# Query tiles, gates and output parts moved between the steps of the last attention of a two-block model

## The chip, the cores and the metric

The kernel runs on one core of a Trainium2 chip. The time is the device time of one execution in microseconds (us). TensorE multiplies matrices, VectorE, ScalarE and GpSimd do elementwise work, and SyncE (SP) and ScalarE issue the transfers. In the profile TensorE is PE (its weight loads PEld), VectorE DVE, ScalarE ACT, GpSimd POOL.

## The reference, cut to what matters

Two transformer layers of one model are followed by an mLSTM layer and an attention layer of a second one, all in fp32 on 512 tokens of width 1024 and 256 context tokens. The change touches the last layer alone, the attention `attn_mixer` (no context output is needed there):

```python
q, k, v, z = split(h @ w_in)               # 16 query heads, 4 key heads, of 64
q, k = rms_norm(q) , rms_norm(k)           # per head, with gains
ql, kl = rope(ql) * scale, rope(kl)
s_loc = where(|qpos - kpos| <= 128, ql @ kl.T, -inf)
s_ctx = ql @ kc.T                          # 256 context keys
p = softmax over [s_loc, s_ctx, sink]      # the sink adds to the sum alone
y = (p @ [v, vc]) * silu(z) @ w_out
x = x + gate * y
```

## The kernel before

Every engine has a program of its own, written out in order, and waits on semaphores that count what the other engines have finished; `at(engine, name)` is the count that stands for a named event, `claim` makes TensorE wait until the last reader of a PSUM bank is done. A projection in fp32 is three fp32r matmuls (high by high, high by low, low by high part), so each unit of weights (128x1024) is loaded by SP, rounded to its high part by ScalarE (`split`, L1293) and subtracted to its low part by GpSimd (L2778). Three units of split weights are held at a time (`SPLIT_SLOTS`): a split waits until TensorE has used the third unit before it.

The attention has four groups g, one for each key head, and 16 steps r in a group: step s = 16 g + r takes one head and one block of 128 queries (four heads of one block in a row). In step s TensorE computes the scores of unit s (L1237, L1238), transposes the probabilities of unit s-3 (L1253), and in every fourth and first step multiplies four units by the values (L632, fp32) and spreads the reciprocals (L1245). VectorE adds the mask and takes the row minimum (L2721), ScalarE takes the exponential with its row sum (L1984); the transposed probabilities are copied out of PSUM by VectorE for even units (L2739) and by ScalarE for odd ones (L1998). `gated` on VectorE (L2698 to L2706) multiplies the spread reciprocal, the value product and the gate. The sink exponential comes once in four steps (L2729, L1991), its sum and reciprocal at L2748 to L2752.

Into these steps `fill` on TensorE and `follow` on ScalarE and VectorE weave the next group's preparation. In groups 0 to 2 and for n = g+1 they are: four query tiles of 128 tokens (`AQ_STEPS` 0, 1, 2, 4; 24 matmuls of 256 columns each), the key turns (steps 5 and 9), two gates of 512 columns in halves of four k-tiles (`AZ_STEPS` 6, 8, 9, 10), and four query turns (`QT_STEPS` 13, 14, 14, 15; L1162). A query tile is copied by ScalarE (L1827), squared, summed, scaled head by head on VectorE (L2620) and rotated in three parts on all four tiles at once (L2589 to L2596); the turned queries and keys are split into high (L1856, L1850) and low part (L2642, L2633). A gate's silu is made of a copy and an exponential on ScalarE (L1868, L1871), an add of one on GpSimd (L2965), logarithm and exponential on ScalarE (L1878, L1880), and a product on GpSimd (L2971). In group 3 the first half of the output projection fills steps 1, 2, 4, 5, 6, 8, 9, 10 (`AO_STEPS`), for which ScalarE and GpSimd make the high and low part of the gated output (L1886, L2989). After step 63 the second half of the output projection follows.

GpSimd's order for group n is: second unit of gate n, first of query n+1, two adds, second of query n+1, two products, first unit of gate n+1; in the last round the units of the output projection take the place of query and gate n+1, and after it come four low halves of the gated output.

## Time and profile before

| | |
|---|---|
| median of 3 runs | 2458.07 us (2456.03 to 2459.13) |
| profiled execution, its own time | 2458.86 us |
| its span, first to last instruction | 2457.1 us |
| mean granted clock of TensorE | 0.991 |
| last attention, first score to last matmul | from 2164.9 to about 2453.9 us |

The span is what the trace shows; the device time lies 1.8 us around it. A busy time of PE counts the pipelined end of each matmul, so the distance from start to start is what a matmul costs in a row. A granted clock of 1.00 is 2.4 GHz, 0.50 is 1.2 GHz, and a share in between means that a window holds both.

### The profile page before, as it was taken

The numbers are of one execution on the slowest core, as the hardware profiler recorded it, in microseconds if no ns is written. First come the engines' busy times: TensorE is split into PE (matmuls) and PEld (weight loads), VectorE is DVE, ScalarE is ACT, GpSimd is POOL, SyncE is SP. The second block draws the span as 40 slices with busy tenths as digits, with TensorE's granted clock in tenths as the row PEclk, the third lists the DMA queues.
The fourth block names the chain that finished last, engine by engine and source line by source line (L and its number), as shares of the span: only waits on it lengthen the run. The fifth ranks groups of instructions, "written<-read, shape, count | busy, mean of one in ns | idle before, by whom it ended". The sixth has DMA issues, their size and how long they took to land.

```text
span 2457.1 us, 32452 instructions
## 1 busy us (share of the span) xinstructions
PE 2397.0 (98%) x12352; PEld 2002.5 (81%) x12352; DVE 1302.2 (53%) x2362; ACT 1019.5 (41%) x1789; POOL 955.6 (39%) x519
## 2 busy tenths in 40 slices
PE   9999999999999999999999999999999999999998
PEld 8877788888888678888888888888888888887766
DVE  5466588631255667875026733831462552656563
ACT  5564544432345544444334323331322332464552
POOL 5232444765523235466653223222323224331231
PEclk9999999999999999999999999999999999999999
DMA  5212255222321124632321111121111111211100
GB/s 199 69 39 78 103 180 189 96 94 95 137 64 53 69 78 154 205 121 99 105 95 52 61 44 52 52 69 61 52 60 44 52 52 52 64 52 35 35 18 35
DMA packets 54585, 200.48 MB, mean 82 GB/s; under 512 B 6176, under 2 KB 6176, under 8 KB 53664
## 3 DMA queue, kind: packets, MB, share of 16 engines
q1 hardware_dynamic: 52272, 189.27, 22.8%
q10 hardware_dynamic: 2160, 9.15, 1.1%
q8 instruction: 99, 1.62, 0.3%
q14 instruction: 54, 0.44, 0.1%
HBM read 196.29 MB, written 2.10 MB: 81 GB/s over the span
## 4 chain that ended last, share of the span: by engine, by line
PE 87%; DVE 6%; ACT 3%; issue 2%; POOL 1%; DMA 0%; SPq 0%; DVEq 0%; ACTq 0%; POOLq 0%
PE ps L582 28%; PE ps L909 25%; PE ps L602 18%; PE ps L632 7%; PE ps L1040 2%; PE ps L800 2%; PE ps L1253 1%; DVE arena L2072 1%; PE ps L816 1%; POOL wl L2778 1%; DVE ps L2050 1%; PE ps L1238 0%; PE ps L1237 0%; ACT kh L1417 0%; DVE arena L2296 0%
## 5 line engine op out<-in xcount | busy, mean ns | idle before, releaser
L2778 POOL TENSOR_TENSOR wl<-wring,wh 128x1024 fp32r<-128x1024 f32 (+1 forms) x305 | 735.5, 2412 | 1169.0 <-ACT wh L1293 1137.1
L1293 ACT ACTIVATE wh<-wring 128x1024 fp32r<-128x1024 f32 (+1 forms) x305 | 316.5, 1042 | 429.2 <-PE ps L909 223.9
L582 PE MATMUL ps<-hh,wh 128*128 128x512 f32 x768 | 300.1, 391 | 2.2 <-POOL wl L2778 2.2
L582 PE MATMUL ps<-hh,wl 128*128 128x512 f32 x768 | 298.8, 389 | 0.0
L582 PE MATMUL ps<-hl,wh 128*128 128x512 f32 x768 | 298.8, 389 | 0.0
L602 PE MATMUL ps<-hh,wh 128*128 128x512 f32 (+1 forms) x472 | 200.2, 424 | 5.7 <-DVE hl L2759 2.4
L602 PE MATMUL ps<-hh,wl 128*128 128x512 f32 (+1 forms) x472 | 187.5, 397 | 0.0
L602 PE MATMUL ps<-hl,wh 128*128 128x512 f32 (+1 forms) x472 | 186.6, 395 | 0.0
L582 PEld LDWEIGHTS ps<-hh,wh 128*128 128x128 f32 x768 | 144.1, 188 | 33.9 <-DVE arena L2287 1.7
L582 PEld LDWEIGHTS ps<-hl,wh 128*128 128x128 f32 x768 | 144.2, 188 | 30.5 <-issue 0.5
L582 PEld LDWEIGHTS ps<-hh,wl 128*128 128x128 f32 x768 | 144.1, 188 | 29.8
L1580 ACT ACTIVATE arena<-ps,prmt 128x512 f32<-128x512 f32 x88 | 68.6, 779 | 226.7 <-DVE ps L2050 226.7
L632 PE MATMUL ps<-arena 128*128 128x64 f32 (+2 forms) x624 | 138.4, 352 | 11.3 <-DVE arena L2256 4.6
L909 PE MATMUL ps<-hh,wh 128*128 128x512 f32 x368 | 144.3, 392 | 0.0
L909 PE MATMUL ps<-hl,wh 128*128 128x512 f32 x368 | 144.3, 392 | 0.0
L909 PE MATMUL ps<-hh,wl 128*128 128x512 f32 x368 | 143.1, 389 | 0.0
L582 PE MATMUL ps<-gu_h,wh 128*128 128x512 f32 x352 | 137.2, 390 | 0.0
L582 PE MATMUL ps<-gu_h,wl 128*128 128x512 f32 x352 | 137.0, 389 | 0.0
L582 PE MATMUL ps<-gu_l,wh 128*128 128x512 f32 x352 | 136.9, 389 | 0.0
L1531 ACT ACTIVATE arena<-arena,st 128x128 f32<-128x128 f32 (+3 forms) x128 | 71.8, 561 | 139.8 <-DVE st L2227 139.0
L2072 DVE CUSTOM_DVE_ANT_0 arena<-arena,ps 128x1024 f32<-128x1024 f32 x96 | 117.3, 1222 | 13.9 <-DVE mod L2072 0.3
L632 PEld LDWEIGHTS ps<-arena 128*128 128x128 f32 x624 | 88.0, 193 | 37.6 <-issue 20.2
(373 smaller groups left out, 5613.2 us busy)
## 6 DMA issues: line engine op xcount, KB each, us to landing
wring<-wts SPq DMA_DIRECT2D x290, 512.0 KB, 3.4
arena<-wts SPq DMA_DIRECT2D x48, 512.0 KB, 4.0
wring<-wts SPq DMA_DIRECT2D x16, 384.0 KB, 3.0
xL<-xt SPq DMA_DIRECT2D x4, 512.0 KB, 6.8
arena<-tab SPq DMA_DIRECT2D x1, 2048.0 KB, 16.4
arena<-cv ACTq DMA_DIRECT2D x2, 1024.0 KB, 4.9
arena<-tab ACTq DMA_DIRECT2D x1, 2048.0 KB, 9.8
out_t<-xL ACTq DMA_DIRECT2D x8, 256.0 KB, 2.0
```

Of the source, the lines that this page charges most:

```text
L582: mm = nc.tensor.matmul(o[0], a, b, start=start and k == first and j == 0, stop=stop and k == last and j == 2)
L602: mm = nc.tensor.matmul(dst, a, b, start=start and x == 0 and i == 0 and j == 0, stop=stop and x == len(us) - 1 and i == kn - 1 and j == 2)
L632: last = nc.tensor.matmul(dst, a, b, start=start and i == 0, stop=stop and i == len(pairs) - 1)
L800: last = nc.tensor.matmul(ps[:, s % 3, 0:ke], a, b, start=x == 0, stop=x == len(bs) - 1 and kind != "fox")
L816: last = nc.tensor.transpose(ps[:, 3 + tb, 128 * j:128 * j + 128], sbuf[:, u % 4, 128 * j:128 * j + 128], idn)
L909: mm = nc.tensor.matmul(dst, a, b, start=x == 0 and i == 0 and j == 0, stop=x == len(us) - 1 and i == kn - 1 and j == 2)
L1040: last = nc.tensor.matmul(l, x, y, start=s == 0 and i == 0, stop=s == NA - 1 and i == 2)
L1293: nc.scalar.activation(wh[:, sn % SPLIT_SLOTS, :kn * w], raw(u)[:, :kn * w], ACT.Copy).then_inc(act_done, tick("act", ("hi", u)))
L1531: nc.scalar.activation(sbuf[:, s % 4, 0:ke], sbuf[:, s % 4, 0:ke], ACT.Exp, scale=-1.0, bias=mx1[:, s % 16:s % 16 + 1], accum_out=rs1[:, s ...
L1580: nc.scalar.activation(yb[:, m % 3, :], ps[:, up_bank(m), :], ACT.Identity, scale=conv[:, l, 2, m:m + 1], bias=conv[:, l, 3, m:m + 1]).the ...
L2072: V.tensor_tensor_reduce(out=ada_dump, in0=raw(u), in1=silu_c[j], scale=1.0, scalar=0.0, op0=ALU.mult, op1=ALU.add, accum_out=modv[:, laye ...
L2778: G.tensor_tensor(wl[:, sn % SPLIT_SLOTS, :kn * w], raw(u)[:, :kn * w], wh[:, sn % SPLIT_SLOTS, :kn * w].bitcast(F32), ALU.subtract).then_inc(
```

## The change

The work of the last attention is put at other steps, some of it in other pieces; what is computed stays.

- TensorE's query tiles move a group ahead: those of group n+2 stand at steps 9, 10, 13, 14 of group n (bank 6 and 7 in turn). Three tiles of group 1 come before step 0, the fourth in step 0.
- The queries are squared, summed, rooted, rotated, turned and split in two pairs of tiles instead of in one piece or four. Pair 0 is turned at step 8 (9 in group 2), pair 1 at 12. The key turns stand at steps 1 and 5.
- The gates stand at steps 1 to 6; those of the last group are cut into quarters of two k-tiles, at steps 1, 2, 5, 6, 9, 10 of group 2.
- The output projection's first half goes to steps 46, 49, 50, 53, 54, 57, 58, 61, with two banks in turn, and one part of its second half to step 62. Step 46 now waits for the low half 3.
- ScalarE copies the transposed probabilities ahead of the step's exponential instead of behind it.
- Row sum and sink exponential lie side by side in pairs, and one reduction takes the place of the addition.
- GpSimd's order changes with the splits; the product of gate 7 comes behind the four low halves.

```diff
-AQ_STEPS, AZ_STEPS, AO_STEPS = (0, 1, 2, 4), (6, 8, 9, 10), (1, 2, 4, 5, 6, 8, 9, 10)
-QT_STEPS = {13: [(0, 7)], 14: [(1, 6), (2, 7)], 15: [(3, 7)]}
+AZ_STEPS = ({1: ((0, 0, 4),), 3: ((0, 4, 8),), 5: ((1, 0, 4),), 6: ((1, 4, 8),)},
+            {1: ((0, 0, 4),), 2: ((0, 4, 8),), 5: ((1, 0, 4),), 6: ((1, 4, 8),)},
+            {1: ((0, 0, 4),), 2: ((0, 4, 6),), 5: ((0, 6, 8), (1, 0, 2)), 6: ((1, 2, 4),), 9: ((1, 4, 6),), 10: ((1, 6, 8),)})
+AQ_STEPS = {9: (0, 6), 10: (1, 7), 13: (2, 6), 14: (3, 7)}
+AK_STEPS = {1: 0, 5: 1}
+AQ1_BANKS = (6, 4, 5, 6)
+QT_STEPS = ({8: (0, 7), 12: (1, 7)}, {8: (0, 7), 12: (1, 7)}, {9: (0, 6), 12: (1, 7)})
+AO_STEPS = {46: (0, 7), 49: (1, 6), 50: (2, 7), 53: (3, 6), 54: (4, 7), 57: (5, 6), 58: (6, 7), 61: (7, 6)}
...
-        ars = st[:, 112:128]
-        aes = st[:, 128:144]
+        asum = st[:, 112:144].rearrange("p (h x) -> p h x", x=2)
+        ars, aes = asum[:, :, 0], asum[:, :, 1]
...
+            gate_part(0, 1, 0, KT, 7)
+            for t in range(NT - 1):
+                query_tile(1, t, AQ1_BANKS[t])
... TensorE, fill(s)
+                if s == 0:
+                    query_tile(1, NT - 1, AQ1_BANKS[NT - 1])
+                if g < AT_KV - 2 and r in AQ_STEPS:
+                    query_tile(g + 2, *AQ_STEPS[r])
+                if s in AO_STEPS:
+                    m, b = AO_STEPS[s]
                     if m == 0:
                         pe.wait_ge(pool_done, at("pool", "aol", 3))
+                    claim([b], "dve", "xa0", m)
+                    out_part(m, b, 0, ("xa0", m), start=True, stop=True)
+                if s == 62:
+                    pe.wait_ge(pool_done, at("pool", "aol", 5))
+                    begin_out(2)
... ScalarE, follow(s)
+                    if r in AK_STEPS: high_keys(n, AK_STEPS[r], 6)
+                    for i, _, k1 in AZ_STEPS[g].get(r, ()):
+                        if k1 == KT: gate_parts(2 * n + i, 7)
+                    if r == 2: root_of_queries(n, 1)
+                    if r in QT_STEPS[g]: high_queries(n, *QT_STEPS[g][r])
+                if g < AT_KV - 2:
+                    if r in AQ_STEPS: take_query(n + 1, *AQ_STEPS[r])
+                    if r == 3: split(("aq", n + 1), first)
+                    if r == 7: split(("aq", n + 1), second); gate_inverse(2 * n)
+                    if r == 9: split(("az", n + 1), first)
+                    if r == 10: gate_inverse(2 * n + 1)
+                    if r == 11: square_queries(n + 1, 0)
+                    if r == 14: split(("az", n + 1), second)
+                    if r == 15: square_queries(n + 1, 1); root_of_queries(n + 1, 0)
+                elif g == AT_KV - 2:
+                    if r == 3: split(("ao", 0, 0))
+                    if r in (11, 13): high_gated(r - 11); high_gated(r - 10)
+                    if r == 6: split(("ao", 1, 0))
+                    if r == 9: gate_inverse(2 * n)
+                    if r == 10: split(("ao", 2, 0))
+                    if r == 14: gate_inverse(2 * n + 1)
... VectorE, follow(s)
+                    if r == 1: sum_queries(n, 1); scale_queries(n, *range(4))
+                    if r - 1 in AK_STEPS: low_keys(n, AK_STEPS[r - 1], 6)
+                    if r == 2: scale_queries(n, *range(4, 8))
+                    if r == 3: rotate_queries(n, 0, 0)
+                    if r == 5: rotate_queries(n, 0, 1); rotate_queries(n, 0, 2)
+                    if r == 6: scale_queries(n, *range(8, 15))
+                    if r == 7: scale_queries(n, 15)
+                    if r == 10: the three parts of rotate_queries(n, 1, part)
+                    if r - 1 in QT_STEPS[g]: low_queries(n, *QT_STEPS[g][r - 1])
+                if g < AT_KV - 2 and r == 14: sum_queries(n + 1, 0)
...
-                    V.tensor_tensor(arc[:, c4], ars[:, c4], aes[:, c4], ALU.add)
+                    V.tensor_reduce(arc[:, c4], asum[:, c4, :], AX_X, ALU.add)
... GpSimd
+            for n in range(1, AT_KV - 1):
+                add_one(2 * n)
+                split(("aq", n + 1), slice(0, 1))
+                add_one(2 * n + 1)
+                split(("aq", n + 1), slice(1, 2))
+                times(2 * n)
+                split(("az", n + 1), slice(0, 1))
+                times(2 * n + 1)
+                split(("az", n + 1), slice(1, 2))
+            split(("ao", 0, 0)); add_one(6)
+            split(("ao", 1, 0)); times(6)
+            split(("ao", 2, 0)); add_one(7)
             for m in range(4):
                 low_gated(m)
+            times(7)
```

(In the diff some bodies are joined to one line and waits that only guard a buffer are left out.)

## Rows read from the trace of the kernel before

**Rows 1.** The page's head and busy times, whole span.
```profile
span 2457.1 us, 32452 instructions
PE 2397.0 (98%) x12352; PEld 2002.5 (81%) x12352; DVE 1302.2 (53%) x2362; ACT 1019.5 (41%) x1789; POOL 955.6 (39%) x519
```

**Rows 2.** Windows: length, busy us of PE, PEld, DVE, ACT, POOL; clock, DMA, GB/s.
```profile
2211.68:2224.56 12.88, 8.18 (x41) 5.80 (x39) 9.37 (x22) 6.71 (x15) 4.82 (x3) 0.87 0.24 82
2277.95:2292.40 14.45, 9.67 (x41) 6.42 (x39) 9.87 (x22) 7.27 (x17) 4.83 (x3) 0.76 0.20 73
2292.40:2345.25 52.85, 52.29 (x312) 42.42 (x309) 31.51 (x81) 27.82 (x59) 11.18 (x6) 1.00 0.06 21
2345.25:2360.04 14.79, 10.53 (x41) 6.83 (x39) 10.82 (x22) 9.05 (x20) 8.64 (x6) 0.66 0.20 72
2411.21:2422.40 11.19, 8.51 (x47) 5.77 (x45) 5.59 (x15) 3.61 (x9) 0.00 (x0) 1.00 0.00 0
2435.85:2457.10 21.25, 15.64 (x61) 12.32 (x60) 8.15 (x12) 1.48 (x2) 2.40 (x1) 0.92 0.26 99
```

**Rows 3.** Chain of work, parts of the last attention: start, us, what.
```profile
2205.35 0.17 PE ps L1237
...
2208.20 0.12 PE ps L1237
...
2209.12 0.55 PE ps L1253 x5
2209.67 2.59 PE ps L632 x6
...
2228.73 2.87 PE ps L602 x24
...
2402.12 2.76 PE ps L602 x12
```

**Rows 4.** Waits of PE from 2110 us on: us in total, times, longest.
```profile
PE ps L1162 <- DVE norm_sq L2596: 7.0, 3, 2.3
PE ps L1253 <- ACT arena L1998: 5.5, 6, 1.5
```

**Rows 5.** Groups of DVE by form from 2110 us on: busy, mean ns; idle before.
```profile
L2721 DVE CUSTOM_DVE_ANT_0 arena<-ps,arena,st 128x640 f32<-128x640 f32 x32 | 28.2, 881 | 22.9 <-PE ps L1238 13.1 <-PE ps L1245 9.7
...
L2620 DVE SCALAR_TENSOR_TENSOR norm_sq<-norm_sq,st,prmt 128x64 f32<-128x64 f32 x64 | 13.1, 278 | 0.7 <-ACT st L1844 0.6
...
L2698 DVE TENSOR_TENSOR arena<-ps,arena 128x256 f32<-128x256 f32 x16 | 6.7, 420 | 9.5 <-PE ps L1245 9.5
...
L2633 DVE TENSOR_TENSOR akl<-ps,akh 64x512 fp32r<-64x512 f32 x8 | 5.5, 687 | 7.6 <-ACT akh L1850 7.4
...
L2748 DVE TENSOR_TENSOR st<-st 128x4 f32<-128x4 f32 x16 | 2.4, 152 | 0.0
...
L2651 DVE TENSOR_REDUCE st<-arena 128x8 f32<-128x512 f32 x1 | 0.7, 675 | 0.0
```

**Rows 6.** Groups of ACT by form from 2110 us on.
```profile
L1293 ACT ACTIVATE wh<-wring 128x1024 fp32r<-128x1024 f32 x25 | 26.2, 1050 | 12.2 <-PE ps L582 6.5 <-PE ps L602 5.6
...
L1868 ACT ACTIVATE arena<-ps 128x512 f32<-128x512 f32 x6 | 3.6, 599 | 10.3 <-PE ps L602 10.3
```

**Rows 7.** Groups of POOL by form from 2110 us on.
```profile
L2778 POOL TENSOR_TENSOR wl<-wring,wh 128x1024 fp32r<-128x1024 f32 x25 | 60.5, 2418 | 217.9 <-ACT wh L1293 217.5
L2965 POOL TENSOR_SCALAR arena<-arena 128x512 f32<-128x512 f32 x6 | 11.5, 1923 | 29.7 <-ACT arena L1871 29.7
```

**Rows 8.** Timeline of POOL, then of DVE: start, us, what, idle before.
```profile
2255.05 2.36 POOL L2778 TENSOR_TENSOR wl<-wring,wh 128x1024 fp32r<-128x1024 f32 x1 [33.90 <-ACT wh L1293]
...
2354.88 4.09 POOL L2989 TENSOR_TENSOR hl<-arena,hh 128x512 fp32r<-128x512 f32 x3
...
2255.07 2.36 DVE L2729 TENSOR_TENSOR st<-st 128x4 f32<-128x4 f32 x1
...
2279.54 1.56 DVE L2595 TENSOR_TENSOR norm_sq<-norm_sq,norm_tmp 128x512 f32<-128x512 f32 x1
```

More of the change, by code:

```diff
@@ L1165, in gate_half, with query_tile @@
-            def gate_half(g, i, half, b):
+                    for t in range(2):
+                        last = nc.tensor.transpose(ps[:, b, 256 * x + 128 * t:256 * x + 128 * t + 128],
+                                                   atq[:, 2 * pair + t, 128 * x:128 * x + 128], idn)
+                last.then_inc(pe_done, tick("pe", ("qt", g, pair)))
+            def query_tile(g, t, b):
+                us = views(("aq", g))
+                claim([b], "act", "aq", g, t)
+                product(ps[:, b, 0:256], lat_toks(t), us, ("aq", g, t),
+                        *([("used", x[0]) for x in us] if t == NT - 1 else []))
@@ L1895, in _ @@
                 take_query(0, t, t)
-            square_queries(0)
+            for pair in range(2):
+                square_queries(0, pair)
             split(("akv", 1), first)
@@ L1899, in _ @@
                 take_kv(0, x)
-            root_of(aqs, ("qss", 0), "qrs", 0)
+            for pair in range(2):
+                root_of_queries(0, pair)
             take_kv(0, 3)
@@ L1919, in _ @@
             high_keys(0, 1, 1)
-            for t in range(NT):
-                high_queries(0, t, 2 + t)
+            for pair in range(2):
+                high_queries(0, pair, 2 + pair)
             split(("aq", 1), second)
@@ L1932, in follow @@
                         split(("ao", 3, 0))
-                    if r == 6:
+                    if r in (5, 6):
+                        high_gated(r - 1)
+                    if r == 5:
                         split(("ao", 0, 1))
-                        high_gated(4)
-                        high_gated(5)
-                    if r in (9, 11):
-                        split(("ao", (r - 7) // 2, 1))
-                    return
-                n = g + 1
-                ahead = ([(("aq", n + 1), first), (("aq", n + 1), second), (("az", n + 1), first)] if n < AT_KV - 1
-                         else [(("ao", j, 0), slice(None)) for j in range(3)])
@@ new lines, in rotate_queries @@
+            def rotate_queries(g, pair, part):
+                c = slice(2 * pair, 2 * pair + 2)
+                x = nsq_t[:].rearrange("p (t h d) -> p t h d", t=NT, d=64)[:, c]
+                t1, t2 = [atmp[:, i, 256 * pair:256 * pair + 256].rearrange("p (t h d) -> p t h d", t=2, h=4)
+                          for i in range(2)]
+                turn_pairs(x, acos[:, c], asin[:, c], t1, t2, part)
+                if part == 2:
+                    names[("dve", ("qr", g, pair))] = counts["dve"]
```

315 lines of the change are left out of this document (169 added, 146 removed).

## The prediction

> **What bounds the kernel now.** I began with the page's head: TensorE is busy for 2397.0 us of a span of 2457.1 [rows 1], so only work or idle time of TensorE can move the end. That 98% is a mean over stages, and the change touches one, the last attention. I cut it into windows at the score matmuls and set beside each window the time that its matmuls need when they follow each other without a gap. That spacing is read in the chain of work: a score of 256 columns 0.12 us (of 384: 0.17), a transpose 0.11, an fp32 matmul of the value product 0.43 (each is recorded twice, so one key tile costs 0.86), a projection matmul 0.12 at 256 columns and 0.23 at 512 [rows 3].
>
> The windows split the stage clearly [rows 2]. Steps 16 to 28 and 32 to 44 run gapless: the second of them, 52.85 us, has PE busy for 52.29 at clock 1.00. Steps 13 to 15 of groups 0, 1 and 2 begin only 38 matmuls each (the rows count three more that reach over an edge; 12 scores 1.4, 22 transposes 2.4, 4 value matmuls 1.7: 5.6 us), but last 12.88, 14.45 and 14.79 us, at clocks 0.87, 0.76 and 0.66. Together 42.1 us for 16.7 of work: **25.4 us lost**. The waits name the cause: TensorE stands at the query transposes until VectorE has rotated the queries (L1162 on L2596, 7.0 us in three waits), then at the probability transposes for ScalarE's copies (L1253 on L1998, 5.5 us in six) [rows 4], and the half clock of 1.2 GHz that follows stretches the rest. Steps 61 to 63 have the same illness: 44 matmuls that begin there, worth 8.2 us, take 11.19 [rows 2], **3.0 us lost**. So 28.4 us can be had here; matmul work is neither added nor taken away.
>
> **What the change does to each step.** Query tiles and gates were done at steps 0 to 10 of the group that precedes their use, and steps 13 to 15 were left bare. Now the query tiles of group n+2 stand at steps 9, 10, 13, 14, the gates at 1 to 6, the turned queries at 8 and 12. With the spacings above TensorE's steps 0 to 15 of group 1 cost
>
> before: 6.8, 3.8, 3.8, 2.6, 6.1, 1.5, 3.7, 2.9, 6.0, 4.1, 3.9, 2.9, 4.0, 1.2, 1.5, 2.9;
> after: 3.9, 4.1, 3.6, 2.6, 3.2, 4.0, 3.7, 2.9, 3.7, 4.0, 4.0, 2.9, 4.5, 3.9, 3.9, 2.6
>
> (a query tile 24 x 0.12 = 2.87, a gate half 12 x 0.23 = 2.76). They add up to 57.7 and 57.5, the same but for rounding.
>
> Can the others follow? VectorE, step by step, from [rows 5] less the 0.08 by which neighbours overlap: bias and minimum 0.80 at 640 columns (0.68 at 512), a copy about as long, three products of the gated output 1.35 (0.42 each and their waits), reciprocals 0.7; the moved work is sixteen head scalings 0.21 apart, key parts 1.24 and 0.86, rotations, low halves. After: 2.0, 3.4, 2.8, 2.3, 2.2, 3.8, 3.1, 2.0, 2.2, 3.5, 3.3, 1.7, 2.0, 3.4, 1.3, 1.5, in all 40.5: below TensorE at every step, by 0.2 at least. ScalarE was busy for 27.8 and 9.1 us in steps 32 to 47 [rows 2] and does the same work in no more instructions: about 37 of 57. So TensorE stays the bound if nothing stands still in the wrong place, and the 28.4 us are the gross gain. A query tile is moved three times into the stretch ahead of step 0 (8.6 us there, 8.6 less in steps 0 to 2): no sum changes, and the half of the tile's weights that is last split is due about when the first half of tile 0 has run; cost 0, up to 1 us if it is late.
>
> **Forms that the trace does not show.** Half a rotation (128x256, both inputs in SBUF) lies between nothing but issue and the 128x512 of 0.69; by the 64x512 key part of 0.69 and the reduction of half the queries, 0.68 [rows 5], time goes with the elements of a partition, so I take 0.42, 12 instead of 6 of them: +0.7 us of VectorE in a group, hidden under 17 us of room. The pair sums by TENSOR_REDUCE (128x4 from 128x8) lie between the old addition, 0.15, and the 0.68 of a 512-element reduction; being nearest in elements to the former I take 0.16, cost 0, and at the other end 16 x 0.5 = 8 us of VectorE, still hidden. Query halves now go as 64x512 (the key part's 0.69 and ScalarE's like form) in half as many instructions: a small saving off the path. Loads keep their order and their rule (slot free after the low half of five units before) and SP's queue is passed by nothing; the windows show DMA shares of 0.26 at most [rows 2], so the earlier splits of the output weights find them landed; a load that did not would cost its landing time once.
>
> **Where waits come back.** I walked steps 0 to 48 through the three queues.
> Step 5 of group 0: VectorE does a key part and four scalings in step 2 before it minimises step 3, about 3 us late; ScalarE then has exponential 3, gate 2 (1.2) and a split (1.05) in front of the copy of unit 1, for which the transposes of step 5 wait [rows 5, 6]: **2.4 us**, 0 if VectorE is earlier.
> Steps 12 and 28: VectorE's six rotations of pair 1 (step 10) meet GpSimd's split of the next gate's first half, started by ScalarE in step 9. A VectorE op on two SBUF inputs stands still meanwhile: L2729, 4 elements wide, took 2.36 us beside a split that began 0.02 us earlier [rows 8]. So the rotations end 2.4 us late, minimum 11 and copy 8 behind them, and the transposes of step 12 wait 1.1: **2.2 us** in two groups, between 0 and 4.8.
>
> The Trainium skill (SBUF — State Buffer, Who interferes with whom) says that VectorE with two SBUF inputs and a GpSimd instruction that reads SBUF take turns as wholes, and that TENSOR_REDUCE never contends on trn2. The 2.36 us agree with the first; by the second the pair sums would save up to 2.2 us for each old addition that met a split, and the sum would be lower by that; but the addition took 0.15 us on the mean of 16 [rows 5], so by the trace they save nothing.
>
> Step 46: the first output part now waits here for low half 3. After the last gate piece (step 42) come, in GpSimd's order, gate readings on ScalarE 1.2, split 1.05, low split 2.42, add-one 1.92, four low halves at 4.09/3 = 1.36 apart [rows 6 to 8]: 12.0 us. TensorE has 2.9 + 4.5 + 1.0 + 1.0 = 9.4 until then: **2.7 us**. Queued behind it are the scores of step 47 and all else on TensorE. In the tail, behind a wait, the clock was 0.92 and 61 matmuls took 15.6 us where 13.9 are due [rows 2]; a little over half of that 1.7 is added here, **1.0**.
> The subtraction ahead of the sink exponential (L2729, every fourth step) can again fall just behind a split, at step 15 in groups 0 and 1 and at step 7 in group 2: price up to 2.4 each, of which a copy and a transpose pass on part; **1.6** in all.
> Bank 6 is shared by value product, key turn and query tiles, and freed by VectorE about 1.0 us after the product, while TensorE needs it after 0.9 to 1.5: **0.8** over six places.
> Copies ahead of exponentials cost nothing as long as an exponential has its three steps of room; the 0.7 it is delayed is covered by 2.6 us or more of the shortest step.
>
> Sum: 28.4 − 2.4 − 2.2 − 3.7 − 1.6 − 0.8 = 17.7. The profiled execution took 2458.86 us around its span of 2457.1; less 17.7 that is 2441.2. The median of the three runs, 2458.07, lies 0.8 below the profiled execution, so I predict **2440.4**. With none of the new waits 2429.6, with all of them doubled 2451.
>
> **Rivals.** (a) *The waits mostly come back.* VectorE works in order and idles at each gated product until the value product ends (behind which a projection used to stand, and now at steps 0 and 4 none does). If that makes each of three groups lose 3 us more, 2449 to 2451. For it: my margins at bank 6 and 7 are under 1 us. Against: 17 us of room in each group's VectorE.
> (b) *No change that can be told.* A measurement of this kernel tells about 0.2%, 4.9 us. If the bare steps are slow because of the chain score, minimum, exponential, transpose, copy itself, moving matmuls does not help: what steps 13 to 15 gain, steps 0, 4 and 8 lose, which now hold 8.1 us less between them in a group, and we end within 2453 to 2463. Against: step 11 took 2.85 us with the same chain (first scores at 2205.35 and, of step 12, 2208.20 [rows 3]).
> (c) *Slower, by the shared port.* 27 GpSimd ops with two inputs stand in the loop (15 splits, 12 others), and the rotations, scalings and subtractions are now spread over seven steps instead of five, so more of them meet a split. At 2.4 us a meeting that reaches TensorE it is decided from 8 meetings beyond mine; with 12 the time is 2440.4 + 29 = 2469. Against: before, of a group's rotations one was held and reached TensorE, for 0.9 us of 1.56 in step 29 [rows 8].
>
> By the Trainium skill (SBUF — State Buffer, Who interferes with whom) this is the mechanism, and what it makes of the time is the 2469.
>
> **How the numbers follow.** Forecast 0.70 (2432 to 2447), (a) 0.20, (b) 0.04, (c) 0.06. Faster by over 0.2%: 0.90; within: 0.04; slower: 0.06. The range takes the forecast's lower bound short of the no-wait end and most of (a): 2432 to 2450.
>
> **What would show it.** Right: windows at steps 13 to 15 of about 10 us with twice the matmuls and clock near 1.00 (in groups 0 and 1); no wait of TensorE on the rotation; 57 to 60 us for group 1; one wait of TensorE on GpSimd's low half near step 46; waits of transposes on copies at step 5 and 12. Wrong would be: VectorE busy without gaps over a group, long L2729 or rotations beside splits followed by TensorE idle at the same moment, or a wait for query weights ahead of step 0.

## The result, and the profile after

The changed kernel takes 2441.24 us in the median of six runs (2436.94 to 2448.48), beside 2456.98 (2455.28 to 2459.13) for six runs of the kernel before on the same chip: a ratio of 0.9937, 95% interval 0.9922 to 0.9953. The forecast of 2440.4 us, faster, in a range from 2432 to 2450, holds. A later set of five runs (the last experiment) gave a median of 2444.77 (2440.37 to 2448.09), beside 2457.58 for the kernel before; over all eleven it is 2442.57. The gain is 15.7 us by the first set and 12.8 by the later one, where the forecast had 17.7. The profiled execution, 2436.94 us, is the fastest of the eleven, which matters for how its profile is read.

The head and busy times of the page, as [rows 1]:

```profile
span 2435.2 us, 32465 instructions
PE 2382.3 (98%) x12352; PEld 1994.0 (82%) x12352; DVE 1309.6 (54%) x2374; ACT 1017.9 (42%) x1785; POOL 956.8 (39%) x519
```

The share of TensorE is 98% as before, with the same 12352 matmuls, so it says nothing of what was gained. The windows do. Those of the kernel after, in the columns of [rows 2]: steps 13 to 15 of groups 0, 1 and 2, steps 61 and 62, and the last 21.25 us:

```profile
2214.35:2224.46 10.11, 10.11 (x81) 9.39 (x80) 7.04 (x17) 5.82 (x13) 0.62 (x1) 1.00 0.01 2
2273.11:2283.22 10.11, 10.11 (x81) 9.39 (x80) 7.06 (x17) 5.82 (x13) 0.62 (x1) 1.00 0.01 2
2332.14:2344.56 12.42, 9.14 (x46) 7.12 (x44) 6.91 (x17) 6.29 (x12) 4.32 (x4) 0.86 0.00 0
2390.84:2399.40 8.56, 8.54 (x48) 6.90 (x47) 5.28 (x15) 3.40 (x7) 2.39 (x1) 1.00 0.00 0
2413.95:2435.20 21.25, 15.63 (x64) 11.57 (x63) 8.58 (x13) 1.48 (x2) 2.40 (x1) 1.00 0.26 99
```

In groups 0 and 1 the three steps hold 81 matmuls instead of 41 and take 10.11 us instead of 12.88 and 14.45, PE busy throughout at clock 1.00. In group 2 TensorE still stands idle for over 3 us in them, and the clock is 0.86. The waits of TensorE in the whole attention, as [rows 4], show why. Line numbers have moved: in the changed kernel a projection is L608 (L602 before), the value product L638 (L632), a transpose of probabilities L1270 (L1253), its copy L2031 on ScalarE (L1998) and L2809 on VectorE (L2739), a gate's first exponential L1891 (L1871), the low part of queries L2694 (L2642), a low half of the gated output L3047 on GpSimd (L2989) and, in the tail, L2829 on VectorE (L2759).

```profile
PE ps L608 <- POOL hl L3047: 2.6, 1, 2.6
PE ps L638 <- DVE aq_s L2694: 2.4, 1, 2.4
PE ps L608 <- DVE hl L2829: 2.4, 1, 2.4
PE ps L608 <- ACT arena L1891: 2.0, 1, 2.0
PE ps L1270 <- ACT arena L2031: 1.8, 2, 1.5
PE ps L1270 <- DVE arena L2809: 1.5, 3, 0.8
```

No query transpose waits for a rotation any more. In its place stand six smaller causes: step 46 (low half of the gated output), step 43 (value product behind the queries' low part), the tail, step 37 (a gate quarter), step 5, and steps 4, 12 and 28. Three of them were in the forecast (steps 46, 5, and 12 with 28), the tail's wait stood there before as well (L602 on L2759, 2.4 us), and steps 37 and 43 were not foreseen.

With each matmul at the spacings of [rows 3] (and 0.23 for 512 columns) every step has a length without waits; what the trace shows beyond it is called lost. Summed over steps, in us lost:

| | before | after, profiled | after, another execution (experiment 12) |
|---|---|---|---|
| group 0, 1 | 10.5, 10.5 | 3.2, 1.4 | 4.7, 1.4 |
| group 2 | 10.3 | 12.7 | 16.9 |
| group 3 to step 62 | 2.2 | 1.9 | 1.9 |
| from step 63 on | 6.3 | 3.0 | 4.4 |
| all | 39.9 | 22.2 | 29.3 |

From the key turns to the last matmul the stretch took 295.57 us before and 278.37 after: 17.2 less, where the forecast had 17.7. The spans differ by 21.9; the other 4.7 lie ahead of the last attention, at places that the change does not touch, and are no part of its gain: by its first key turn the execution before was that much behind already (it had been at 1.2 GHz for 20.5 us by then, the one after for 6.8).

Nor is all of the 17.2 the change's own. The stretch from the key turns on as a window, in the columns of [rows 2]: before, after, and after in the other execution of the table (the last experiment):

```profile
2157.91:2453.48 295.57, 273.73 (x1457) 214.63 (x1455) 171.39 (x406) 142.66 (x299) 72.31 (x37) 0.96 0.10 34
2153.19:2431.56 278.37, 263.70 (x1456) 209.03 (x1455) 174.65 (x411) 141.07 (x292) 72.91 (x37) 0.99 0.11 36
2157.16:2442.70 285.54, 271.02 (x1456) 214.50 (x1455) 174.58 (x411) 141.00 (x292) 72.75 (x37) 0.96 0.10 35
```

At the same clock as before, 0.96, the change saves 10.0 us; the other 7.2 of the profiled execution come with a clock of 0.99.

### The profile page after: what moved, and what is told of

Read it like the earlier page. It is cut to its first block, busy times and chain, and to the rows that moved or that the text cites. A ratio compares the mean times of both kernels' runs of the same rounds, so it can differ in the third digit from the quotient of the medians.

```text
span 2435.2 us, 32465 instructions
## 1 busy us (share of the span) xinstructions
PE 2382.3 (98%) x12352; PEld 1994.0 (82%) x12352; DVE 1309.6 (54%) x2374; ACT 1017.9 (42%) x1785; POOL 956.8 (39%) x519
## 4 chain that ended last, share of the span: by engine, by line
PE 89%; DVE 6%; ACT 2%; issue 1%; POOL 1%; DMA 0%; DVEq 0%; ACTq 0%; POOLq 0%
PE ps L588 29%; PE ps L915 25%; PE ps L608 18%; PE ps L638 7%; PE ps L1046 2%; PE ps L806 2%; PE ps L1270 1%; DVE arena L2118 1%; PE ps L822 1%; POOL wl L2848 1%; PE ps L1255 1%; PE ps L1254 1%; DVE ps L2096 0%; DVE arena L2342 0%; PE ps L1041 0%
## 5 line engine op out<-in xcount | busy, mean ns | idle before, releaser
L608 PE MATMUL ps<-hh,wh 128*128 128x512 f32 (+1 forms) x472 | 197.8, 419 | 10.2 <-POOL hl L3047 2.6
L608 PE MATMUL ps<-hh,wl 128*128 128x512 f32 (+1 forms) x472 | 186.1, 394 | 0.0
L608 PE MATMUL ps<-hl,wh 128*128 128x512 f32 (+1 forms) x472 | 185.4, 393 | 0.0
L638 PE MATMUL ps<-arena 128*128 128x64 f32 (+2 forms) x624 | 135.0, 346 | 12.1 <-DVE arena L2302 4.5
L638 PEld LDWEIGHTS ps<-arena 128*128 128x128 f32 x624 | 86.7, 191 | 36.9 <-issue 19.1
## 6 DMA issues: line engine op xcount, KB each, us to landing
arena<-tab SPq DMA_DIRECT2D x1, 2048.0 KB, 17.2
```

Source lines behind the costliest of these rows:

```text
L608: mm = nc.tensor.matmul(dst, a, b, start=start and x == 0 and i == 0 and j == 0, stop=stop and x == len(us) - 1 and i == kn - 1 and j == 2)
L638: last = nc.tensor.matmul(dst, a, b, start=start and i == 0, stop=stop and i == len(pairs) - 1)
```

## The experiments

The theory after the result: the bare steps lost time through the rotation that the turns stood for, that is gone, and what is left in the changed kernel are single waits, each with its own late engine or held bank, followed at times by a half-clock stretch. The rival theories, one for each part, stand in the expectations. A single run of a kernel in which such waits are left tells little by its total (the same kernel spreads over 11.5 us, last experiment), so the first seven experiments, one profiled run each, are judged by their waits. The times of the kernel before on the same chips were 2461.1 us (first four, one run), 2457.85 (next four) and 2457.58 (last four).

The expectations set bounds for the stretch from the first key turn to the last matmul. Here it is for each profiled execution, with the part of it in which TensorE was granted 1.2 GHz:

| | stretch, us | at 1.2 GHz, us |
|---|---|---|
| before | 295.57 | 23.9 |
| after | 278.37 | 3.4 |
| 1 e1_copy_behind | 284.39 | 13.7 |
| 2 e2_add | 279.83 | 6.8 |
| 3 e3_high_early | 280.80 | 10.2 |
| 4 e4_low_first | 285.49 | 20.5 |
| 5 e5_quarter_later | 278.53 | 6.8 |
| 6 e6_split_later | 279.91 | 10.2 |
| 7 e7_halves | 279.14 | 10.2 |
| 8 e8_spread | 274.11 | 6.8 |
| 9 e9_low_ahead | 269.81 | 0.0 |
| 10 e10_part_47 | 268.96 | 0.0 |
| 11 e11_short_tiles | 274.63 | 6.8 |
| 12 e12_after_again | 285.54 | 20.5 |

A projection matmul of 512 columns takes 0.43 us at this level instead of 0.23, so up to half of the last column is time lost, and it must come off before two stretches are compared.

**1. The copy behind the exponential again** (e1_copy_behind).

```diff
-                if 0 <= u < nu and u % 2:   # copy of unit s-3, ahead of exponential s
...
+                if 0 <= u < nu and u % 2:   # the same copy, behind the exponential and the sink's
```

> The changed kernel with one part undone: ScalarE's copy of the transposed probabilities stands behind the step's exponential again. Measured is the stretch from the first key turn to the last matmul, 278.4 us in the changed kernel. Theory 1 (the copies' place is worth little, since the moved matmuls now cover a copy that comes late): the stretch stays within 3 us, and TensorE's waits for these copies, 1.8 us in two waits, grow to 5 us at most. Theory 2 (much of the gain comes from this order): the waits for the copies come back in many steps and the stretch grows by 5 us or more.

2445.09 us. The copies are waited for in three places instead of two; in step 5 the wait is 2.28 instead of 1.47 us, longer by the 0.83 of the exponential that now stands in front:

```profile
PE ps L1270 <- ACT arena L2044: 3.6, 3, 2.3
```

One of the others shortens the wait in step 43 from 2.4 to 1.6, so some 1.0 us of waiting is added in all. The stretch grows by 6.0, past theory 2's bound of 5, but the rest of it is clock: in this execution a half-clock stretch of 6.8 us follows step 5 and one of 3.4 lies in the tail. The order of copy and exponential is worth about 1 us of waits, as theory 1 has it.

**2. The addition instead of the reduction** (e2_add).

```diff
-V.tensor_reduce(arc[:, c4], asum[:, c4, :], AX_X, ALU.add)
+V.tensor_tensor(arc[:, c4], ars[:, c4], aes[:, c4], ALU.add)
```

> The changed kernel with one part undone: row sum and sink exponential are added by a two-input addition again instead of a reduction over pairs. Theory 1 (the trace): nothing changes, the stretch from the first key turn to the last matmul stays within 1 us of 278.4; where the addition meets GpSimd's split in step 5 it waits 1.5 us, but the copy behind it waited for the same split anyway. Theory 2 (the Trainium skill, SBUF - State Buffer, Who interferes with whom: a reduction never contends, two inputs do): held additions reach TensorE and the stretch grows by 1.5 to 3 us.

2440.08 us, and the list of TensorE's waits is that of the changed kernel to 0.1 us. The form itself differs. VectorE's sums by form, this kernel first, then the changed one:

```profile
L2818 DVE TENSOR_TENSOR st<-st 128x4 f32<-128x4 f32 x16 | 4.0, 252 | 0.0
```

```profile
L2818 DVE TENSOR_REDUCE st<-st 128x4 f32<-128x8 f32 x16 | 2.4, 152 | 0.0
```

At the new places one addition of the 16 is held up, in step 5, for 1.74 us instead of 0.15; the reduction never is. But these 1.6 us are not on TensorE's path. That the stretch is 1.5 longer, more than theory 1 allows, goes with a half-clock stretch of 3.4 us behind the wait in step 37, which the profiled execution of the changed kernel does not have there.

**3. The high parts 2 and 3 in step 43** (e3_high_early).

```diff
-                    if r in (11, 13):
-                        high_gated(r - 11)
-                        high_gated(r - 10)
+                    if r == 11:
+                        for m in range(4):
+                            high_gated(m)
```

> The changed kernel, with ScalarE's high parts 2 and 3 of the gated output made in step 43 beside 0 and 1 instead of in step 45. Theory 1 (step 46 waits because GpSimd's low halves 2 and 3 start late behind ScalarE): the wait of TensorE on the low half, 2.6 us, falls below 0.8, the half-clock period behind it goes, and the stretch from the first key turn to the last matmul falls from 278.4 to 273.5 to 276. Theory 2 (GpSimd's own queue of split, add-one and four low halves sets step 46): the wait stays above 1.5 us and the stretch above 276.5.

2440.79 us. GpSimd's four low halves now follow each other without a gap, and the wait for them is gone. But step 46 still waits 1.3 us, which the list puts down to nothing ("issue"). The two timelines name it, TensorE's first and then VectorE's:

```profile
2341.75 0.47 PE L608 MATMUL ps<-hh,wh 128*128 128x512 f32 x1 [1.26 <-issue]
```

```profile
2340.24 1.41 DVE L2694 TENSOR_TENSOR aq_s<-ps,aq_s 64x512 fp32r<-64x512 f32 x2
```

VectorE's low parts of query pair 1 end at 2341.65 and free bank 7; the output part that claims bank 7 begins 0.10 later. The next bound of step 46 is a bank. The stretch was expected at 273.5 to 276 and is 280.8, which misses it: the half clock behind step 46 is gone, but in this execution it follows the waits in steps 37 and 43 and in the tail.

**4. In step 42 the low parts ahead of the rotations** (e4_low_first).

```diff
+                    if r - 1 in QT_STEPS[g]:
+                        low_queries(n, *QT_STEPS[g][r - 1])
                     if r == 10:
                         for part in range(3):
                             rotate_queries(n, 1, part)
-                    if r - 1 in QT_STEPS[g]:
-                        low_queries(n, *QT_STEPS[g][r - 1])
```

> The changed kernel, with VectorE taking the low parts of query pair 0 ahead of the rotations of pair 1 in step 42 instead of behind them. Theory 1 (step 43 waits because bank 6, which the value product needs, still holds the turned queries that VectorE reads after six rotations): the wait of 2.6 us at step 43 falls below 0.5, and the stretch from the first key turn to the last matmul falls by 0.5 to 2.5 us (part is given back at step 46, whose low halves do not come earlier). Theory 2 (the wait is for the probability copies of units 38 and 39): it stays above 2 us.

2444.96 us. The wait in step 43 is gone, and the transposes of step 44 wait 2.5 us instead. The list names ScalarE (L1906); the timeline of VectorE shows the copy of unit 40, which holds the transposes' bank, ending at 2332.32, 0.15 ahead of the transposes, behind the rotations and two instructions that were held:

```profile
2326.11 1.21 DVE L2635 TENSOR_TENSOR norm_tmp<-norm_sq,arena 128x256 f32<-128x256 f32 x1
...
2330.21 1.38 DVE L2799 TENSOR_TENSOR st<-st 128x4 f32<-128x4 f32 x1
2331.51 0.81 DVE L2809 COPY arena<-ps 128x640 f32<-128x640 f32 x1
```

Theory 1 is right on the bank, but the gain that it expected is not there (285.5 us, 20.5 of it at half clock): in either order step 42 puts six rotations, a low part and a copy of VectorE into 2.6 us of TensorE. Two of the rows shown are held beside GpSimd instructions, the rotation of 1.21 us (0.42 for the others) and the subtraction of 1.38 (0.16 at most places). These 2.0 us may be most of the wait; no run here tried that by itself.

**5. The first quarter of gate 7 in step 38** (e5_quarter_later).

```diff
-5: ((0, 6, 8), (1, 0, 2)), 6: ((1, 2, 4),)
+5: ((0, 6, 8),), 6: ((1, 0, 4),)
```

> The changed kernel with one step of the last gates moved: the first quarter of gate 7 is multiplied in step 38 instead of in step 37, where it follows the last quarter of gate 6 in the same PSUM bank 7. Theory 1 (step 37 waits because the bank can only be written again when ScalarE has read gate 6 twice): TensorE's wait of 2.0 us on ScalarE's gate reading goes, and no other wait of steps 36 to 42 grows by more than 0.5. Theory 2 (VectorE is behind in steps 36 to 40 in any case): the wait comes back at the probability transposes of steps 38 to 40, 1.5 us or more.

2436.89 us. The wait of 2.0 us in step 37 falls to 1.0, now in step 38: there too ScalarE reads gate 6 out of bank 7 by copy and exponential before gate 7 may be written. About 1 us is gained in waits, half of what theory 1 expected, and no other wait grows.

**6. The next gate's first split in step 12** (e6_split_later).

```diff
-                    if r == 9:
-                        split(("az", n + 1), first)
...
+                    if r == 12:
+                        split(("az", n + 1), first)
```

> The changed kernel, with ScalarE's split of the next gate's first unit in step 12 instead of step 9 of groups 0 and 1, so that GpSimd's part no longer runs beside VectorE's rotation in step 10. Theory 1 (the shared turn of VectorE and GpSimd delays rotation, copy and the transposes of steps 12 and 28): the first rotation of step 10 takes 0.4 instead of 2.6 us and the waits at steps 12 and 28, 0.55 us each at the transposes, go; the stretch from the first key turn to the last matmul falls by 1 to 2 us, unless the half clock falls otherwise. Theory 2 (these waits come from VectorE's amount of work): the rotation is short, but the waits stay above 0.3 us.

2441.07 us. The first rotation of step 10 in group 0 takes 0.42 us, beside 2.64 in the changed kernel, where GpSimd's split began 0.05 us ahead of it and took 2.41. The timelines of the changed kernel, VectorE and then GpSimd, and of VectorE in this one:

```profile
2204.24 2.64 DVE L2635 TENSOR_TENSOR norm_tmp<-norm_sq,arena 128x256 f32<-128x256 f32 x1
```

```profile
2204.19 2.41 POOL L2848 TENSOR_TENSOR wl<-wring,wh 128x1024 fp32r<-128x1024 f32 x1 [4.70 <-ACT wh L1308]
```

```profile
2206.87 0.42 DVE L2635 TENSOR_TENSOR norm_tmp<-norm_sq,arena 128x256 f32<-128x256 f32 x1
```

The waits in steps 12 and 28 are gone: 0.55 us each. The chain split, rotation, minimum, copy, transpose is shown. The stretch does not fall by the 1 to 2 us expected; it has 10.2 us at half clock instead of 3.4.

**7. The last gates in halves** (e7_halves).

```diff
-1: ((0, 0, 4),), 2: ((0, 4, 6),), 5: ((0, 6, 8), (1, 0, 2)), 6: ((1, 2, 4),), 9: ((1, 4, 6),), 10: ((1, 6, 8),)
+1: ((0, 0, 4),), 2: ((0, 4, 8),), 5: ((1, 0, 4),), 6: ((1, 4, 8),)
```

> The changed kernel with one part undone: the gates of the last group in halves of four k-tiles at steps 33, 34, 37, 38 as in the other groups, instead of quarters up to step 42. Theory 1 (the quarters only shift waits): the 2.0 us at step 37 go, steps 41 and 42 lose 1.4 us of work each and their waits grow by about as much, and the stretch from the first key turn to the last matmul stays within 2.5 us of 278.4. Theory 2 (the quarters carry part of the gain, as they fill steps that VectorE's rotations make long): the stretch grows by 3 us or more.

2441.55 us. Step 37 does not wait any more and step 40 neither, but steps 41 to 43, with the quarters taken out of them, lose 6.8 us instead of 3.2: TensorE waits for ScalarE's copy (2.0) and then for the low part (1.5), with a half-clock stretch of 6.8 us. The stretch of 279.1 is within theory 1's bound. The quarters shift waits; they neither make nor remove them.

**8. All five moves** (e8_spread): edits 3, 5 and 6, the low parts of step 42 ahead of the rotation, the three rotations of pair 1 in group 2 spread over steps 40 to 42, and the split of step 3 in step 4.

```diff
... (of the five moves, the rotations alone)
+                    if r == 10 and g < AT_KV - 2:
+                        for part in range(3):
+                            rotate_queries(n, 1, part)
+                    if 8 <= r <= 10 and g == AT_KV - 2:
+                        rotate_queries(n, 1, r - 8)
```

> The changed kernel with five moves at once: high parts 2 and 3 of the gated output in step 43; in group 2 the three rotations of pair 1 in steps 40, 41 and 42 and the low parts of pair 0 ahead of the last of them; first quarter of gate 7 in step 38; split of the next gate's first unit in step 12 of groups 0 and 1; split of the next query's first unit in step 4 instead of 3. Theory 1 (what is left of the gross gain lies in waits each set by one badly placed instruction: 2.0 at step 37, 0.9 at 40, 2.6 at 43, 2.7 and the half clock behind it at 46, 0.6 each at 12 and 28, about 1 at step 5): the stretch from the first key turn to the last matmul falls from 278.4 to 267 to 272, the median time to 2428 to 2435. Theory 2 (VectorE's and ScalarE's amount of work sets group 2, so that a wait removed comes back in the next step): the stretch stays above 274.

2437.02 us in the median of four (2436.18 to 2437.49), ratio 0.9919 [0.9902, 0.9935]. Theory 1's ranges are missed, 2428 to 2435 by the median and 267 to 272 by the stretch, whose 274.1 lies just above theory 2's bound. The single waits did go: steps 5 and 43 lose 0.9 us at most, steps 12, 28 and 44 next to nothing. What they give is partly lost again in step 46, which TensorE now reaches earlier than GpSimd's low halves:

```profile
PE ps L608 <- POOL hl L3049: 2.9, 1, 2.9
```

With 6.8 us of half clock behind it that step loses 6.7 us, more than the 5.4 of the changed kernel.

**9. As 8, with the low halves ahead of gate 7's add of one** (e9_low_ahead).

```diff
-            add_one(7)
             for m in range(4):
                 low_gated(m)
+            add_one(7)
             times(7)
... ScalarE: gate_inverse(2 * n + 1) of group 2 at r == 15 instead of 14
```

> All five moves, and on GpSimd the four low halves of the gated output ahead of the add of one of gate 7 (1.92 us), whose logarithm and exponential go from step 46 to 47. Theory 1, GpSimd's own chain now sets step 46: its low halves begin 2.2 us sooner, TensorE's wait there falls from 3.1 to about 0.9 us and the half-clock stretch behind it (6.8 us long, 2.7 us lost) goes: 2437.0 - 2.2 - 2.7 = 2432. Theory 2, the wait is passed on to the next engine and the half clock stays: a wait of 1.5 us or more in step 46 or 47, 2435 to 2437.

2432.06 us (2430.29 to 2432.83), ratio 0.9897 [0.9883, 0.9911], as theory 1 has it, and no half clock is left in the stretch. The wait in step 46 is 1.3 instead of the 0.9 expected, and it is not GpSimd's chain but the bank of experiment 3: the low halves end at 2332.49, VectorE's low parts at 2332.81, and the output part begins 0.10 later. From the timelines of GpSimd, VectorE and TensorE:

```profile
2326.93 5.56 POOL L3049 TENSOR_TENSOR hl<-arena,hh 128x512 fp32r<-128x512 f32 x4
```

```profile
2331.40 1.41 DVE L2694 TENSOR_TENSOR aq_s<-ps,aq_s 64x512 fp32r<-64x512 f32 x2
```

```profile
2332.91 0.47 PE L608 MATMUL ps<-hh,wh 128*128 128x512 f32 x1 [1.27 <-POOL hl L3049]
```

**10. As 9, with the first output part in step 47** (e10_part_47).

```diff
-AO_STEPS = {46: (0, 7), 49: (1, 6), ...}
+AO_STEPS = {47: (0, 7), 49: (1, 6), ...}
```

> As the run before, and the first output part in step 47 instead of 46, so that step 46 has one score and its transposes alone (1.0 us). Theory 1, only the low halves hold TensorE there: 1.0 us more room, the wait is gone, 0.9 below the run before, 2431. Theory 2, two bare steps (45, 46) are paid for by the chain score, minimum, exponential, transpose: transposes of steps 47 to 49 wait 1 us or more on an exponential or a copy, and the time is the same as or above the run before.

2431.16 us (2429.44 to 2431.65), ratio 0.9893 [0.9880, 0.9907]: the fastest version, 13.6 us below the changed kernel in the same set of runs (2444.77), though hardly to be told from 9. Of steps 45 to 47 two waits are left, on an exponential (0.7, as in the changed kernel and in 9) and on a copy (0.4). Two bare steps in a row cost only the latter, and the wait on bank 7 is gone: theory 1, though what was waited for was the bank and not the low halves. All steps from 0 on lose 12.7 us.

**11. Short query tiles in steps 13 and 14** (e11_short_tiles): three quarters of the matmuls of tiles 2 and 3 in groups 2 and 3 are left out.

```diff
                 us = views(("aq", g))
+                if g >= 2 and t >= 2:
+                    us = [(u, o, 1, [w[:, 0:1, :] for w in v]) for u, o, n, v in us]
```

> The changed kernel, where query tiles 2 and 3 of groups 2 and 3 (steps 13 and 14 of groups 0 and 1) leave out three quarters of their matmuls (6 instead of 24, so the queries are wrong there): steps 13 and 14 become as bare as before the change, 1.7 instead of 3.9 us of work each, but no rotation is due in them. 4 x 18 x 0.12 = 8.6 us of work are left out. Theory 1, what cost time in the bare steps before was the rotation that the turns stood for and the half clock behind it: all 8.6 us are saved, 2432.5. Theory 2, the chain score, minimum, exponential, transpose, copy cannot go faster than some 3 us a step, and a bare step waits for it: less than half is saved, 2437 or more, with transposes waiting on copies in steps 14 to 17 and 30 to 33.

2437.87 us (2435.01 to 2439.31). Neither theory gives the number. Steps 13 to 15 of groups 0 and 1, in the columns of [rows 2]:

```profile
2217.70:2225.15 7.45, 6.23 (x45) 5.11 (x44) 7.04 (x17) 5.36 (x11) 0.15 (x1) 1.00 0.01 2
2273.81:2281.29 7.48, 6.25 (x45) 5.12 (x44) 7.05 (x17) 5.38 (x11) 0.18 (x1) 1.00 0.00 0
```

They take 7.5 us instead of 10.1, so 5.3 of the 8.6 are saved. The rest is not the waiting of transposes on copies that theory 2 expected; these wait as long as in the changed kernel, 0.8 us in steps 6 to 31. In both groups tile 3 stands until VectorE's low parts of query pair 1 have freed bank 7:

```profile
2222.11 0.38 PE L608 MATMUL ps<-wh,hh 128*128 128x256 f32 x1 [1.22 <-DVE aq_s L2696]
```

So the chain from score to copy does go at 1.8 to 3.4 us a step, and VectorE, busy for 7.04 of 7.45 us, is here the next bound. The bare steps before were not slow by the chain as such; that leaves the rotation due in them, with the copies and exponentials late behind it. Matmuls placed there hide VectorE's work.

**12. The changed kernel once more** (e12_after_again), unaltered.

> The changed kernel unaltered, once more, on the same chip as the three others. Theory 1: median 2441, single runs from 2437 to 2449, and the half-clock stretches stand behind the same waits of 1.6 to 2.7 us (steps 5, 37, 43, 46) but not behind the same ones in every execution. Theory 2: the spread was that of one chip: all runs within 2 us of each other.

2444.77 us in the median of five (2440.37 to 2448.09), ratio 0.9948 [0.9936, 0.9960]. Its profiled execution took 2448.09 us, 11.2 more than the one shown above, and TensorE's waits are the same to 0.2 us. The windows of steps 5, 37 to 38, 43 to 44, 46, and from step 63 on, first of the profiled execution above, then of this one:

```profile
2182.43:2188.16 5.73, 4.26 (x25) 3.60 (x24) 4.53 (x10) 4.53 (x10) 4.32 (x2) 1.00 0.00 1
2299.74:2309.05 9.31, 7.30 (x39) 5.72 (x37) 5.97 (x16) 4.34 (x10) 3.12 (x2) 1.00 0.19 58
2321.64:2332.14 10.50, 7.77 (x38) 4.88 (x36) 7.86 (x14) 7.20 (x15) 7.60 (x5) 1.00 0.15 51
2333.15:2342.33 9.18, 5.90 (x25) 4.59 (x23) 3.97 (x10) 5.00 (x10) 3.81 (x3) 0.81 0.00 0
2397.71:2435.20 37.49, 31.87 (x137) 23.07 (x135) 12.71 (x24) 4.64 (x10) 3.79 (x2) 1.00 0.15 56
```

```profile
2186.42:2193.65 7.23, 5.76 (x26) 4.87 (x24) 5.30 (x13) 4.53 (x10) 4.29 (x2) 0.76 0.11 32
2305.24:2316.13 10.89, 8.88 (x38) 7.08 (x37) 6.36 (x18) 4.35 (x10) 3.12 (x2) 0.84 0.15 50
2328.60:2341.85 13.25, 10.52 (x38) 6.58 (x36) 7.85 (x14) 7.20 (x15) 8.09 (x5) 0.74 0.13 41
2342.87:2351.78 8.91, 5.64 (x24) 4.37 (x23) 3.96 (x10) 5.00 (x10) 3.81 (x3) 0.84 0.00 0
2407.45:2446.40 38.95, 33.26 (x137) 24.12 (x135) 12.71 (x24) 4.64 (x10) 3.78 (x2) 0.96 0.14 54
```

Behind the same waits the clock is 1.00 in one execution and 0.74 to 0.84 in the other in three of the four stretches of steps; step 46 is slowed in both. Theory 1 holds, but for a median 3.8 above its own. The lengths differ by 1.50 + 1.58 + 2.75 − 0.27 + 1.46 = 7.0 us, nearly all of the 7.2 by which the stretch from the key turns to the last matmul is longer (285.54 to 278.37). The other 4 of the 11.2 lie ahead of the attention, where this execution has 17.1 us at half clock and the first 6.8. Experiments 9 and 10, where these waits are gone or down to 1.3 us and only the tail's is as long as before, spread over 2.5 and 2.2 us.

## Why the prediction was right, point by point

**The bound and the gross gain.** The bare steps were to lose nothing once they had work in them, and in groups 0 and 1 that held (steps 13 and 14 lose 0.1 us together). The rotation as the cause held as well: VectorE does it steps ahead, no transpose waits on it, and experiment 11 shows that the steps could even be bare without the chain holding them for as long as before. But up to 10 of the 25.4 us were half clock (20.5 us in steps 14 to 47), and that part need not stay away: the other execution of the changed kernel has as much of it at new places.

**Steps 61 to 63 and the tail.** The 3.0 us predicted in steps 61 to 63 came: with projection matmuls in steps 61 and 62 these two waits of the kernel before are gone.

```profile
2414.44 0.74 PE L1253 MATMUL ps<-prmt,arena 128*128 128x128 f32 x5 [1.18 <-ACT arena L1984]
...
2417.15 0.63 PE L1253 MATMUL ps<-prmt,arena 128*128 128x128 f32 x4 [1.50 <-ACT arena L1998]
```

The loss from step 63 on fell from 6.3 to 3.0; half of this is the second of these waits, and half was not in the forecast: the clock behind the tail's wait (2.4 us as before) is 1.00 instead of the 0.92 of [rows 2]. That half is luck of the execution; in the other one, with the clock at 0.96, the loss is 4.4.

**Step 5.** 2.4 us predicted, by VectorE's late minimum and ScalarE's queue. Measured 1.6 in step 5 and 0.8 in step 4, both behind VectorE's late minimum of step 3: 2.4. (The kernel before lost 0.9 in step 4 too, where the transposes followed those of step 3 with only the scores in between; the gross gain below counts it.)

**Steps 12 and 28.** The mechanism was right in each link (experiment 6), the size twice too large: 0.55 us a group instead of 1.1.

**Step 46.** Predicted 2.7 of wait and 1.0 of clock, by GpSimd's chain without a break. Measured: 0.7 at the transposes, a wait of 2.6, and 1.8 of clock: the spacing of the projection matmuls behind the wait is 0.43 us instead of 0.23. The wait has the right size by luck, and by another path: GpSimd stood idle for 2.5 us between low halves 1 and 2, because ScalarE makes the high parts 2 and 3 only in step 45. The timeline of GpSimd in the changed kernel:

```profile
2329.96 2.69 POOL L3047 TENSOR_TENSOR hl<-arena,hh 128x512 fp32r<-128x512 f32 x2
2335.15 2.68 POOL L3047 TENSOR_TENSOR hl<-arena,hh 128x512 fp32r<-128x512 f32 x2 [2.51 <-ACT hh L1906]
```

Without this gap GpSimd's chain takes the 12.0 us predicted and ends at 2335.3; but TensorE, late from step 43, reached the output part only then, so the chain by itself would have cost nothing. Once the gap and the add of one are out of the way (experiments 3 and 9), bank 7 is next.

**Sink subtraction and bank 6.** 1.6 predicted for the subtraction; measured about 0.9 in step 40, behind a subtraction held for 1.29 us in step 39, one of the places named. 0.8 predicted for bank 6 over six places; measured 0.2 to 0.3 in each of steps 17, 21, 33, 49, 53, 57 and 61, 1.7 in all.

**What was missed.** Two waits that no term of the sum held, both for a PSUM bank whose reader is late. From the timeline of TensorE in the changed kernel, step 37 and step 43:

```profile
2305.14 0.50 PE L608 MATMUL ps<-hh,wh 128*128 128x512 f32 x1 [1.98 <-ACT arena L1891]
...
2325.86 1.95 PE L638 MATMUL ps<-arena 128*128 128x512 f32 x4 [2.41 <-DVE aq_s L2694]
```

In step 37 the last quarter of gate 6 and the first of gate 7 stand back to back in bank 7, so ScalarE must read gate 6 twice in between. In step 43 the value product claims bank 6, which in group 2, and only there, holds the query turn of pair 0 from step 41; VectorE reads it behind the six rotations, one of which is held for 1.1 us (1.50 instead of 0.42) beside GpSimd's product of gate 6. Its row on VectorE's timeline, then GpSimd's:

```profile
2321.97 1.50 DVE L2639 TENSOR_TENSOR norm_sq<-norm_sq,arena 128x256 f32<-128x256 f32 x1
```

```profile
2321.92 1.28 POOL L3041 TENSOR_TENSOR arena<-arena 128x512 f32<-128x512 f32 x1 [8.96 <-ACT arena L1900]
```

The walk through the queues priced bank 6 by what frees it after a value product and did not follow the query turn that group 2 puts there. The text named the margin of banks 6 and 7 as what speaks for rival (a); the rival itself, 3 us more in each of three groups, did not come: group 2 alone loses more than before (12.7 against 10.3).

**Why the total fits.** The new losses sum to 2.4 + 1.1 + 5.1 + 0.9 + 1.7 + 2.0 + 2.4 = 15.6 us in the profiled execution, against 10.7 predicted, and the steps' gross gain was larger too: 39.9 lost before and 22.2 after leave 17.7 (17.2 from the key turns on, since 0.5 was added ahead of step 0), so 33.3 were gained where the forecast had 28.4. Of these 4.9 the tail's clock gave some 1.6, and the rest came from steps outside 13 to 15 of groups 0 to 2, which the forecast took as gapless and which lost up to 0.9 us each (steps 0, 4, 24; 0.5 in 6, 7, 22, 38, 39). Two errors of about 5 us took each other away, so that the total fits within 1 us is luck. A run of the median takes 4 to 6 us more than the profiled one (2441.24 and 2442.57 beside 2436.94), and by the last experiment most of such a difference is half clock, in part ahead of the attention; the prediction put 1.0 us on the clock, at one place, where five can show it.

**Rivals.** (b) falls with the result and with experiment 11. (c) did not come: instructions of VectorE held beside GpSimd reach TensorE in steps 12, 28, 40 and, as part of a late queue, 43, which is far from the eight meetings more than foreseen that it needed. Two rows bear on the rule that was weighed there, on VectorE's timeline while GpSimd's split runs from 2185.31 to 2187.71:

```profile
2186.01 0.15 DVE L2818 TENSOR_REDUCE st<-st 128x4 f32<-128x8 f32 x1
...
2186.40 1.46 DVE L2822 COPY arena<-st 128x256 f32<-128x256 f32 x1
```

The reduction runs at its usual 0.15 us and the copy between two SBUF places behind it takes 1.46 instead of 0.29. That the reduction is not held is what the Trainium skill (SBUF — State Buffer, Who interferes with whom) states, and the trace agrees; by experiment 2 it saves 1.6 us of VectorE and nothing of the time.

**The signs.** Those named for right came: 10.11 us with twice the matmuls, 58.76 us for group 1, one wait on the low half in step 46, waits on copies in steps 5 and 12. Of those named for wrong two came in small: held subtractions and rotations with TensorE idle behind them (steps 12, 28 and 40: 2.0 us, where 3.8 were priced in), and a wait for query weights ahead of step 0, 0.2 us.

## What to carry to other kernels

When work is moved into idle steps, follow every shared buffer through the new order: for each claim of a bank, who read it last in this very step and group, and what stands ahead of that reader in its queue; both waits that were missed here were such banks. Where the bank of step 46 held TensorE (experiments 3 and 9), the wait list named "issue" or GpSimd, and only the timelines named the reader. A wait of 2 us on the bounding engine costs more than itself, since the clock may drop behind it, so taking most of them away gave 13.6 us (2444.77 to 2431.16) where the waits of TensorE listed for the attention, without the tail's, fell by about 7, and a steadier time. So compare two executions only with their granted clocks beside them: 17.2 us of gain here are 10.0 at equal clock. Look for the next bound behind each one: in step 46 it went from ScalarE's order to GpSimd's order to a bank, and only moving the claim itself ended it.

## What the runs showed of the hardware that was not expected

The same wait is followed by a half-clock stretch (1.2 GHz) in one execution and not in another of the same kernel. Step 5's wait of 1.5 us has one at 2188.5 us in the second execution and none in the first; step 37's wait of 2.0 likewise. The tail's wait of 2.4 us stands in all fourteen profiled executions and has one behind it in five. With five such places (steps 5, 37, 43, 46 and the tail) a kernel spreads from 2436.9 to 2448.5 us, with a mean clock of 0.998 in its fastest run and of 0.994 and 0.992 in its two slowest; the kernel before, whose waits in this attention sum to 21.6 us instead of 14.3, spreads over 4 us in its six runs. What decides between the two in an execution stays open; no run here was made for it.

A copy with one SBUF input and an SBUF output was held by GpSimd's split (1.46 instead of 0.29 us), not only instructions with two inputs.
